# Router and zeroing in a two-block fp32 kernel: choice in two parts, token table from ranks, bf16 one-hot products, zeroing spread over the early weight loads

## The reference, cut to what matters

```python
h = _layer_norm(DEEPNORM_ALPHA * h + mix, ln1_g[l], ln1_b[l])
ffn = _hier_moe(h, w_rg[l], b_rg[l], w_re[l], b_re[l], w1[l], w3[l], w2[l])
...
pg = jax.nn.softmax((xt @ w_rg + b_rg).astype(jnp.float32), -1)
grp = jnp.argmax(pg, -1)                      # 1 of 4 groups
le = (xt @ w_re + b_re).reshape(n_tok, MOE_GROUPS, MOE_EXPERTS_PER_GROUP)
le = jnp.take_along_axis(le, grp[:, None, None], 1)[:, 0]
top_v, top_i = lax.top_k(le, MOE_TOPK)        # 2 of its 8 experts
gate = (p_grp * jax.nn.softmax(top_v, -1)).reshape(-1)
eid = (grp[:, None] * MOE_EXPERTS_PER_GROUP + top_i)
...
hb = jax.nn.silu(xb @ w1[e]) * (xb @ w3[e])   # each token's 2 experts
return hb @ w2[e]
```

## Time and profile before

| what | value |
|---|---|
| median of 3 runs | 2405.24 us (2403.76 to 2407.4) |
| the profiled execution | 2402.03 us, its span 2400.2 us |
| busy: PE, PE weight loads, DVE, ACT, POOL | 2073.0, 1513.7, 917.9, 629.4, 519.6 us |
| mean granted clock of TensorE | 0.927 of 2.4 GHz |
| chain that ended last, by engine | PE 73%, DVE 10%, issue 6%, ACT 5%, SP's queue 3%, POOL 2% |

### The profile page before, as it was taken

The page is one execution under the profiler, slowest core; times in us unless marked ns, Lnnn a source line. Parts: engine busy times, 40 slices in busy tenths (PEclk is TensorE's granted clock), DMA queues, the critical chain, the costliest instruction groups (busy, mean ns, idle before and its releaser), DMA issues.

```text
span 2400.2 us, 24055 instructions
## 1 busy us (share of the span) xinstructions
PE 2073.0 (86%) x10037; PEld 1513.7 (63%) x10037; DVE 917.9 (38%) x1324; ACT 629.4 (26%) x943; POOL 519.6 (22%) x347
## 2 busy tenths in 40 slices
PE   5999597999999787888788864988887888999999
PEld 4878486888897673333333324666664754888787
DVE  6864253443323453111111126764533653222243
ACT  3432232232323300000000012343134752222231
POOL 4532033232232521111111012221022430000021
PEclk8999798999999987988999986999998998999999
DMA  4444822212223437999999963201210232233220
GB/s 149 106 71 122 181 55 59 46 35 71 48 59 122 145 147 278 406 410 405 401 418 407 418 243 137 106 35 45 70 54 9 70 106 93 83 105 105 71 88 36
DMA packets 97834, 360.76 MB, mean 150 GB/s; under 512 B 10155, under 2 KB 34893, under 8 KB 85433
## 3 DMA queue, kind: packets, MB, share of 16 engines
q1 hardware_dynamic: 82224, 330.51, 39.6%
q0 software_dynamic: 8192, 19.00, 2.3%
q10 hardware_dynamic: 7304, 9.66, 1.2%
HBM read 338.42 MB, written 29.10 MB: 153 GB/s over the span
## 4 chain that ended last, share of the span: by engine, by line
PE 73%; DVE 10%; issue 6%; ACT 5%; SPq 3%; POOL 2%; ACTq 1%; DMA 1%; POOLq 0%; DVEq 0%
PE ps L268 69%; PE ps L272 3%; SPq L465 3%; DVE H L258 2%; ACT ST L264 1%; ACT L264 1%; ACT M L265 1%; DVE ST L252 1%; DVE BG L252 1%; DVE sm L2753 1%; DVE M L255 1%; ACT M L264 0%; DVE BG L258 0%; POOL WL L252 0%; DVE WL L252 0%
## 5 line engine op out<-in xcount | busy, mean ns | idle before, releaser
L268 PE MATMUL ps<-W,BG 128*64 128x512 f32 (+1 forms) x800 | 258.7, 637 | 39.4 <-issue 35.0
L268 PE MATMUL ps<-XH,WS 128*128 128x512 f32 x704 | 217.9, 391 | 0.0
L268 PEld LDWEIGHTS ps<-W,BG 128*64 128x64 f32 (+1 forms) x800 | 87.1, 156 | 158.9 <-issue 154.6
L268 PE MATMUL ps<-HTH,WL 128*128 128x512 f32 x448 | 183.0, 409 | 0.0
L268 PEld LDWEIGHTS ps<-ST 128*128 128x128 f32 x1376 | 171.4, 196 | 18.4 <-POOL ST L252 10.2
L268 PE MATMUL ps<-ST 128*128 128x64 f32 (+1 forms) x1376 | 172.0, 278 | 10.0 <-POOL ST L252 8.8
L268 PEld LDWEIGHTS ps<-XH,WS 128*128 128x128 f32 x704 | 133.0, 189 | 27.7
L268 PE MATMUL ps<-XL,WS 128*128 128x512 f32 x352 | 137.8, 392 | 5.6 <-POOL XL L252 5.6
L2020 DVE COPY BG<-ps 128x512 f32<-128x512 f32 x32 | 22.1, 692 | 301.1 <-PE ps L268 301.1
L268 PE MATMUL ps<-X2H,GV 128*128 128x512 f32 (+1 forms) x512 | 131.7, 348 | 0.0
L262 ACT ACTIVATE BG<-ps 128x512 f32<-128x512 f32 x48 | 28.5, 595 | 390.0 <-PE ps L272 336.9
(11 more groups left out here) (356 smaller groups left out, 4286.6 us busy)
## 6 DMA issues: line engine op xcount, KB each, us to landing
W<-in_w SPq DMA_DIRECT2D x42, 2048.0 KB, 26.6
W<-in_w_in SPq DMA_DIRECT2D x27, 2048.0 KB, 13.8
ST<-in_w SPq DMA_DIRECT2D x14, 2048.0 KB, 26.8
U<-in_w SPq DMA_DIRECT2D x14, 2048.0 KB, 27.5
M<-in_w SPq DMA_DIRECT2D x13, 2048.0 KB, 28.1
HT<-in_w SPq DMA_DIRECT2D x13, 2048.0 KB, 28.2
W<-in_w_ffn_in SPq DMA_DIRECT2D x22, 1024.0 KB, 7.6
ypad<-BG SPq DMA_DIRECT2D x47, 256.0 KB, 4.7
```

Source lines behind the costliest of these rows:

```text
L268: return p.e.matmul(o, lhsT=l, rhs=r, start=start, stop=stop, skip_group_check=True)
```

## The change

1. `ypad` is zeroed in 24 DMAs of up to 512 KB from a `z_t` of 128 partitions, a third of them behind each of the weight loads 2, 3 and 4.
2. The norm before the router: statistics of each half are taken as its residual is added; then two passes over 1024 columns on VectorE, (x − mean) · gain and · 1/sd + bias. GpSimd's part goes. TensorE turns tile m−1 between the two halves of tile m. ScalarE evacuates both halves of the last turned tile; logits 2 come before the last turn.
3. The choice runs for tiles 0 to 2 first and for tile 3 after it (`v_choice`). The mask sum, the triangle, the ones and the one-hot matrices are bf16.
4. The token table of blocks 0 to 31 comes from ranks alone: one-hot of rank (ranks of 64 and more match nothing) times the expert mask times token number, in two bf16 parts (partition + 1 and 128 · tile). Rest of the router (gates, overflow blocks, destination rows) comes after it in `v_rows`, and the overflow part of the table in TensorE's block 0 and VectorE's block 1.
5. GpSimd clears `BG[:, 8:16]` behind the store of `h1d`.

```diff
-        z_t = BG[0:BLK, 22:24, :].rearrange("p a b -> p (a b)")
+        z_t = BG[:, 22:24, :].rearrange("p a b -> p (a b)")
...
-        def q_zero():
+        def q_zero(part):
             q.wait_ge(first_done, 2)
-            for b in range(NBLK):
-                q.e.dma_start(ypad[b * BLK:(b + 1) * BLK, :], z_t).then_inc(c_z, 16)
+            for b in range(part, NZ, 3):
+                n = min(P, NBLK * BLK - b * P)
+                q.e.dma_start(ypad[b * P:b * P + n, :], z_t[0:n, :]).then_inc(c_z, 16)
...
-            for n in range(2, 7):
+            for n in range(2, 5):
                 q_weight(n)
-            q_zero()
-            for n in range(7, N_SEC + 2):
+                q_zero(n - 2)
+            for n in range(5, N_SEC + 2):
                 q_weight(n)
...
-                if m:
-                    p_turn("h1", H, 2, m - 1, (4 + 2 * (m % 2), 5 + 2 * (m % 2)))
+                    if m and y == 0:
+                        p_turn("h1", H, 2, m - 1, (4 + 2 * (m % 2), 5 + 2 * (m % 2)))
                 if m > 1:
                     p_logits(m - 2)
+            p_logits(2)
             p_turn("h1", H, 2, 3, (4, 5))
-            p_logits(2)
             p_logits(3)
...
+        def v_ln2(m):
+            o = H[:, m, :]
+            v.wait_ge(*v.now)
+            v.e.bn_aggr(mv[:, m, :], bnst[:, m, :, :].rearrange("p j k -> p (j k)")).then_inc(ln_var)
+            for x in rows2:
+                v.wait_ge(*x)
+            v.wait_ge(ln_var, 9 + m)
+            stt(o, o, mv[:, m, 0:1], rows[:, 0, :], SUB, MUL).then_inc(v.up())
+            v.wait_ge(ln_sd, 9 + m)
+            v.e.reciprocal(rs[:, m:m + 1], sd[:, m:m + 1]).then_inc(v.up())
+            v.wait_ge(*v.now)
+            stt(o, o, rs[:, m:m + 1], rows[:, 1, :], MUL, ADD).then_inc(ln_hi)
...
         def g_router():
-            g.wait_ge(ln_lo, 12)
             g.wait_ge(ln_hi, 12)
             g.e.dma_start(h1d.rearrange("(i p) d -> p i d", p=P), H[:, :, :]).then_inc(c_h1, 16)
+            g.e.memset(BG[0:BLK, 8:16, :], 0.0).then_inc(xg_zero)
...
-            mm(t.at[:, 0:160], su, mf, stop=False)
+            mm(t.at[:, 0:160], sub_, mfb, stop=False)
             for j in range(1, 5):
-                z = mm(t.at[:, 32 * j:160], ones, mf[:, 0:160 - 32 * j], start=False, stop=j == 4)
+                z = mm(t.at[:, 32 * j:160], oneb, mfb[:, 0:160 - 32 * j], start=False, stop=j == 4)
...
             p.wait_ge(row_hot, 1)
-            p.wait_ge(blk_tok, 1)
             for n in range(8):
-                z = mm(t.at[:, 0:NBLK], hot_r[:, n, :], hot_b[:, n, :], start=n == 0, stop=n == 7)
+                for y in range(2):
+                    z = mm(t.at[:, 0:NE], hot_r[:, n, :], mkt[:, y, n // 4, n % 4, :],
+                           start=n + y == 0, stop=n + y == 8)
...
+            v_logits(2)
+            v_choice(0, 3)
+            v_logits(3)
+            v_choice(3, 4)
...
+            tt(v, hot_r.rearrange("p n (y r) -> p n y r", y=2), io64.unsqueeze(1).unsqueeze(1).to_broadcast([P, 8, 2, BLK]),
+               c_rank.rearrange("p c i -> p (c i)").unsqueeze(2).unsqueeze(2).to_broadcast([P, 8, 2, BLK]),
+               ALU.is_equal).then_inc(row_hot)
...
+                if b == 0:
+                    p_over_rows()
...
+                if b == 1:
+                    v_over_rows()
```

More of the change, by code:

```diff
@@ L28 @@
 NBLK = NE + NOVF
+NZ = -(-NBLK * BLK // P)
 ALPHA = 2.0 ** 0.25
@@ L1605, in v_merge, with v_wo @@
             for m in range(NT):
[L1606 to L1613, removed]
+                v_wo(m, 0)
                 if m:
                     turned_out(v, "h1", m - 1, 0)
+                v_wo(m, 1)
+                v_ln2(m)
                 if m > 1:
                     v_logits(m - 2)
+        def v_wo(m, y):
+            t, o = B["wo", m, y], H[:, m, y * 512:(y + 1) * 512]
+            v.wait_ge(*t.full())
+            stt(o, o, ALPHA, t.at, MUL, ADD).then_inc(t.drained)
+            v.wait_ge(*t.free())
+            v.e.bn_stats(bnst[:, m, y, :], o).then_inc(v.up())
+        def v_ln2(m):
[10 more added lines that the diff above has]
+            stt(o, o, rs[:, m:m + 1], rows[:, 1, :], MUL, ADD).then_inc(ln_hi)
         def g_merge():
@@ L1630, in g_merge @@
             low_merged(g)
-            for m in range(NT):
-                g_ln(H, 2, m, 0, 1, rows2)
         def g_add(n):
@@ L1707, in p_router, with p_over_rows @@
             p.wait_ge(row_hot, 1)
+            for n in range(8):
+                for y in range(2):
+                    z = mm(t.at[:, 0:NE], hot_r[:, n, :], mkt[:, y, n // 4, n % 4, :],
+                           start=n + y == 0, stop=n + y == 8)
+            z.then_inc(t.filled)
+        def p_over_rows():
+            t = B.tile("tok2", 7)
+            room(t)
             p.wait_ge(blk_tok, 1)
             for n in range(8):
-                z = mm(t.at[:, 0:NBLK], hot_r[:, n, :], hot_b[:, n, :], start=n == 0, stop=n == 7)
+                z = mm(t.at[0:BLK, 0:NOVF], hot_r2[:, n, :], hot_b2[:, n, :], start=n == 0, stop=n == 7)
             z.then_inc(t.filled)
@@ new lines, in v_router @@
+            v_logits(3)
+            v_choice(3, 4)
+            for c in range(2):
+                ts(v, mkt[:, 0, c, :, :], mk[:, c, :, :], cst[:, C_TOK:C_TOK + 1], None, MUL, None).then_inc(v.up())
+                tt(v, mkt[:, 1, c, :, :], mk[:, c, :, :],
+                   tile1.unsqueeze(2).to_broadcast([P, 4, 32]), MUL).then_inc(v.up())
+            t = B["rank"]
+            v.wait_ge(*t.full())
+            sc = RT[:, 7, 0:256].rearrange("p (c i n) -> p c i n", c=2, i=4)
+            R = t.at[:, 0:128].rearrange("p (i n) -> p i n", i=4)
@@ new lines, in v_router @@
+            cnt = RT[:, 5, 128:160]
+            v.e.tensor_copy(cnt, t.at[:, 128:160]).then_inc(t.drained)
+            tt(v, gx, lg[:, :, 0:4], m8[:, :, 0:1].to_broadcast([P, 4, 4]), SUB).then_inc(rt_in)
+            tt(v, ex, t8[:, :, 1], t8[:, :, 0], SUB).then_inc(rt_in)
+            t = B["tok"]
+            v.wait_ge(*t.full())
+            ts(v, tokf[:, 0:NE], t.at[:, 0:NE], 0.5, float(FAR), ALU.is_lt, MUL).then_inc(v.up())
+            v.wait_ge(*v.now)
+            stt(toki[:, 0:NE], t.at[0:BLK, 0:NE], -1.0, tokf[0:BLK, 0:NE], ADD, ADD).then_inc(t.drained)
@@ L1745, in v_router @@
[L1745 to L1756, removed]
@@ L1786, in v_router @@
-            v.wait_ge(*v.now)
-            for c in range(2):
-                tt(v, mk[:, c, :, :], over4(io32), ei[:, c, :].unsqueeze(2).to_broadcast([P, 4, 32]), ALU.is_equal).then_inc(v.up())
-            v.wait_ge(*v.now)
-            tt(v, ms, mk[:, 0, :, :], mk[:, 1, :, :], ADD).then_inc(ms_done)
-            den = RT[:, 0, 164:168]
             v.wait_ge(rt_out, 1)
@@ L1802, in v_router @@
             tt(v, gt[:, :, 1], gt[:, :, 0], ex, MUL).then_inc(v.up())
[L1803 to L1809 removed]
+            cnt = RT[:, 5, 128:160]
+            nov, ove, ovb, z32 = [RT[:, 4, 336 + 32 * j:368 + 32 * j] for j in range(4)]
             s7, s8 = RT[:, 7, 0:224].rearrange("p (n y) -> p n y", n=32), RT[:, 7, 224:280].rearrange("p (n y) -> p n y", n=8)
             sc = RT[:, 7, 0:256].rearrange("p (c i n) -> p c i n", c=2, i=4)
[L1812 to L1815 removed]
+            v.wait_ge(*B["rank"].free())
             tt(v, s8, c_rank.rearrange("p c i -> p (c i)").unsqueeze(2).to_broadcast([P, 8, 7]),
@@ L1883, in v_router, with v_over_rows @@
             v.e.tensor_copy(rowi, ri).then_inc(v.up())
+        def v_over_rows():
+            ove = RT[:, 4, 368:400]
+            v.wait_ge(*B["tok2"].full())
+            v.e.tensor_copy(toki[:, NE:NBLK], B["tok2"].at[0:BLK, 0:NOVF]).then_inc(B["tok2"].drained)
             v.e.tensor_copy(novf, ove[0:1, 31:32]).then_inc(dst_done)
             v.wait_ge(dst_done, 2)
+            v.wait_ge(*B["tok2"].free())
             v.wait_ge(*v.now)
```

160 lines of the change are left out of this document (88 added, 72 removed).

## The result

| | before | after |
|---|---|---|
| median of the runs | 2404.96 us (2403.76 to 2407.4, 4 runs) | 2386.15 us (2383.23 to 2387.83, 4 runs) |
| profiled execution, its span | 2402.03, 2400.2 us | 2385.46, 2383.6 us |
| mean granted clock | 0.927 | 0.928 |

The ratio is 0.9919 (95% interval 0.9902 to 0.9936): faster, by 19 us where 28 were forecast. A later set of runs of the same changed kernel gave 2380.55, ratio 0.9896 (0.9874 to 0.9919). The range (2368 to 2387) held both; the likeliest case's own range (2372 to 2382) held only the second. The two sets lie 5.6 us apart (0.0023 in the ratio), so a difference of that size between the medians of two variants of the changed kernel settles nothing by itself.

What follows compares the result with a forecast made beforehand. Bound by the expert weights' DMA stream from 960 to 1380 us, elsewhere by TensorE's chain; zeroing 23.3 + router 5.2 − overflow table 0.3 = 28 us, from a 2405.24 median to 2377, range 2368 to 2387.

Steps and rivals of the forecast that it cites:

- likeliest case: Whole kernel: the forecast sum holds, median 2377 us, own range 2372 to 2382; chance 0.62.
- The zeroing, 23.3 us: Zeroing of ypad: with its wait gone, the TensorE point at 293.95 moves to about 270.6; bounds 19.5 and 24.
- The early cost of 0: Weights 2 to 4: zeroing thirds fit the windows between loads, costing 0 us; bounds 0 and 5.
- ScalarE then issues the load of the bias rows ... 7.2 us: After convolution 23: bias rows issued at 262.2 land 7.2 us later, at 269.4, as long as before.
- rival (D): Stall at 242 to 280 partly replaced: convolution 23's chain or bias rows beside weight 7 take 8 us more; 2385, chance 0.08.
- The router, 5.2 us: Router: the h1d store lands near 913.2, so the first gather is issued at 914.0 instead of 919.22.
- The signs named ahead: Profile after: no ypad wait, TensorE busy at 260, last projection near 859.5, gather near 891 just after the store lands.
- (C): Router gives nothing: store lands at 916 or later, or first gather meets traffic; 2382, sign gather after 894, chance 0.13.
- The table: 19.2 us after wo forecast: Router: token table ready near 902, about 19 us after the last projection at 882.8.
- the opposite case (store alone): Router: if the h1d store had the DMA engines to itself, the sum would be 10 us larger.
- (B): Router: the store isn't the last wait, the table rules and gains 15.5 us; 2367, chance 0.10.
- The 0.3 for the overflow table: TensorE block 0: eight small overflow-table matmuls cost 1 to 2 us under the limiting stream; 0.3 charged.

Runs made afterwards that it cites:

- experiment 7: Changed kernel with zeroing from 64 partitions (256 KB DMAs), still a third behind each of weights 2, 3 and 4: 2381.68 us, ratio 0.9909.
- experiment 2: Changed kernel with weight 7 held back until the bias rows have landed: 2373.18 us, ratio 0.9878.
- the router alone: Changed kernel with the earlier zeroing put back (47 DMAs behind weight 6, 64-partition source): 2400.48 us, ratio 0.9981.
- experiment 3: Changed kernel with the h1d store in four 512 KB DMAs, each issued when its tile's norm is done: 2376.88 us, ratio 0.9883.
- experiment 4: Twelve dummy VectorE steps delay the token table: in the changed kernel 2386.73 us, 0.9933; in that kernel with one store DMA per tile 2383.32, 0.9913.
- experiment 6: Kernel before the change with only its h1d store split into one DMA per token tile: 2403.35 us, ratio 0.9998.
- experiment 8: Changed kernel with all three thirds of the zeroing behind weight 5: 2383.25 us, ratio 0.9914.

## Why the prediction was right, and where its sum was off

**The zeroing, 23.3 us: mechanism right, size too large.** No wait for `ypad`, convolution 22 at 247.00 right behind ScalarE (246.28 + 0.69), TensorE busy at 260. The early cost of 0 holds; the slack was even larger than needed (experiment 7). The mis-sized term is "ScalarE then issues the load of the bias rows ... 7.2 us". I took 7.2 from a row of before, where the row shared the engines with a weight issued 11 us ahead of it, and moved weight 7 up to 3.7 us ahead without charging the row for it. It measured 11.7. This is rival (D), which had the place and the cause right, at 2385 and a chance of 0.08; experiment 2 shows it. The forecast itself, 2377, left it out, and the first set's 2386.15 lies in the stated range only because that was drawn just past (D): 0.85 us inside its edge. From d22 to the fourth V evacuation the zeroing part gave 69.1 − 51.5 = 17.6 us; with weight 7 held back it gives 24.0, so the other terms of the 23.3 stand.

**The router, 5.2 us: right.** The gather is 6.2 us nearer to wo; against the end of the projections before it, 0.9 goes off for the moved transposes (a group of 0.87 us stands before the last projection in the chain of after), leaving 5.3. The store was issued 4.67 us after wo (forecast 887.6 − 882.8 = 4.8, before 7.5) and landed after 25.4. The reload comes 5.1 nearer to wo, less 0.9, so 4.2; the runs of the router alone gave 4.6. The difference of 1 us is the first expert's product, 9.41 us against 8.46. TensorE stood still for 14.0 us ahead of the transposes before it, 4.7 before the change; but 9.9 us ahead of them went with 9.78 in the store per tile, so why it is longer stays open. Experiments 3, 4 and 6 show the statement on which the part turned: the store, not the table, is last in the changed kernel, and not before the change.

**The signs named ahead.** The gather was to be issued near 891, and "later than 894" was to mean (C). It was issued at 900.53 (895.44 in the second profile), and yet (C) is wrong: the last projection's evacuation, forecast near 859.5, came at 869.49 (862.97), so the clock time carried the delays of the stages before. From wo to the gather 31.2 us were forecast (914.0 − 882.8) and 31.0 and 32.5 measured. The times could not have told the cases apart: 2382 was (C)'s and 2385 (D)'s, and the two sets lie at 2380.55 and 2386.15. A sign for one stage must be counted from that stage's own start.

**The table: 19.2 us after wo forecast, 20.5 measured,** out of terms that were further off. The choice was done 16.7 us after wo (886.18 against 869.49) where I had 13.8: the cast of `oneb`, which I did not cost, took 4.37 us, the choice stood behind it on VectorE, and the rank product waited for the choice. The rank product took 0.57 (886.24 to 886.81; forecast 1.0) and the token product 0.61 (forecast 1.9). Off the path, none of it counted.

**"By the opposite case (store alone) the sum would be 10 us larger": wrong.** With the store out of the way the gather comes 9.5 us earlier against wo, the reload only 4. I had the row for it, 8.3 us for gathers under load, and used it in rival (C) only; (B), at 2367, took the whole gain. On the store itself, the Trainium skill ("DMA: Bandwidth & Descriptors", Queues, rings and completion order: each engine takes its queues in turn, a packet at a time) fits what the runs show, though none tests it: one 2 MB store beside weights takes 25.4 us, a 512 KB piece of it with no weight beside it 2.9.

**The median.** 17.6 and 4.2 make 22, so 2383; the two sets of runs of the changed kernel lie at 2386.15 and 2380.55. The 0.3 for the overflow table is below what can be seen.

## What to carry to other kernels

When a stall is removed, price the next wait with the neighbours it will have then: here a 512 KB load on the path took 11.7 us instead of 4.1 because a 2 MB load that nobody was waiting for yet had moved to just ahead of it, and holding that load back gave 6.4 us in its stretch. A path made shorter on one branch of a join gains only up to the other branch; issuing the big store in pieces as its rows are final took it off the join. And bulk work with no deadline can go into any window in which the queue and the DMA engines are idle: how fast it ran there did not matter as long as it was out by the next load's turn.

## What the runs showed of the hardware

- The zeroing from 64 partitions moved 210 GB/s, from 128 partitions 415 to 418 GB/s (windows with nothing else in flight, experiments 7 and 8).
- A 512 KB load landed in 4.1 us with no weight ahead of it and in 11.7 behind a 2 MB load issued 3.7 us earlier on another queue (experiment 2).
- A short fp32-to-bf16 cast on VectorE took 4.1 to 4.4 us each time, where an equal one just before took 0.21; it started 0.05 to 0.06 us after GpSimd began to issue a store and ended 0.08 to 0.09 us after the 3.53 us memset that followed.
- The first gather of 64 rows landed in 3.1 us with the engines free, and in 6.9 beside three 512 KB loads of another queue, 8.3 with the tail of a weight as well. Holding those rows back was not tried; with the table last, they are what stands ahead of the first expert next.
- Sixteen bf16 matmuls with 32 columns took 0.61 us, 0.038 each; before, 16 passes in fp32 with 47 columns took 3.62.
